# A one-core fp16x3 transformer kernel: head weight panels split ahead of the norms, the bias folded into the even low parts, and two panels given a seventh home

## The reference, cut to what matters

```python
# first block
h = x
h = h + mixed(rms_norm(h)) @ w_out                      # Hyena and mLSTM mixers
h = h + cross_attention(rms_norm(h), rms_norm(mem), wq, wk, wv, wo)
h = h + square(relu(rms_norm(h) @ ff_w1)) @ ff_w2
x = rms_norm(h, final_norm_g)
# second block, two layers (mixers differ: convolution + window attention, then GLA + MLA)
x = layer_norm(ALPHA * x + mixer(x) @ w_out, ln_mix_g, ln_mix_b)
x = layer_norm(ALPHA * x + (silu(x @ w_gate) * (x @ w_up)) @ w_down, ln_ffn_g, ln_ffn_b)
# layer_norm: ((x - mean) * rsqrt(var + eps)) * g + b ; rms_norm has neither mean nor bias
```

## Time and profile before

| | us |
|---|---|
| median of 3 runs | 2020.98 |
| the runs | 2020.11, 2020.98, 2023.48 |
| the profiled execution, its own time | 2021.97 |
| span of that execution, first to last instruction | 2020.1 |
| TensorE matmul busy | 1970.3 (98%) |
| TensorE weight load busy | 1188.0 (59%) |
| VectorE busy | 939.5 (47%) |
| ScalarE busy | 731.5 (36%) |
| GpSimd busy | 368.9 (18%) |
| mean granted TensorE clock, share of full speed | 0.993 |

### The profile page before, as it was taken

One profiled execution on the slowest core, in us unless ns is written; L12 is line 12 of the kernel. 1 busy time (PEld: TensorE's weight loads), 2 busy tenths in 40 slices (PEclk: granted clock), 3 DMA queues, 4 the chain that ended last, 5 costly groups with the idle time before them and its releaser, 6 DMA issues.

```text
span 2020.1 us, 27357 instructions
## 1 busy us (share of the span) xinstructions
PE 1970.3 (98%) x11550; PEld 1188.0 (59%) x11550; DVE 939.5 (47%) x1254; ACT 731.5 (36%) x1173; POOL 368.9 (18%) x379
## 2 busy tenths in 40 slices
PE   8999999999999999999999999999999999999997
PEld 5655555757664444885576444448766575444466
DVE  6666677645543322254745222222665663222224
ACT  6443312435343331143534222212465543322213
POOL 1011111410132210042016121200610125211100
PEclk9999999999999999999999999999998999999999
DMA  7221100332322333322121333323111022222331
GB/s 244 84 84 63 63 22 21 102 107 105 105 70 98 104 104 104 105 84 105 63 84 63 104 104 104 104 96 113 64 63 57 28 84 101 98 95 103 104 105 42
DMA packets 28228, 179.66 MB, mean 89 GB/s; under 512 B 2960, under 2 KB 7184, under 8 KB 7184
## 3 DMA queue, kind: packets, MB, share of 16 engines
q1 hardware_dynamic: 27312, 170.93, 24.5%
q10 hardware_dynamic: 512, 4.94, 0.7%
q0 software_dynamic: 288, 2.10, 0.3%
HBM read 175.86 MB, written 2.10 MB: 88 GB/s over the span
## 4 chain that ended last, share of the span: by engine, by line
PE 85%; DVE 8%; ACT 3%; POOL 1%; issue 1%; DMA 1%; SPq 0%; ACTq 0%; DVEq 0%
PE psum_a L382 25%; PE psum_a L384 25%; PE psum_a L383 25%; PE psum_a L717 2%; PE psum_b L519 2%; DVE X L1822 1%; DVE RINV L1796 1%; PE psum_a L655 1%; POOL U L2583 1%; DMA W<-weights 1%; PE psum_b L632 1%; PE psum_a L728 1%; ACT W_PARTS L1232 1%; PE psum_b L1057 1%; DVE X L1827 1%
## 5 line engine op out<-in xcount | busy, mean ns | idle before, releaser
L1802 DVE SCALAR_TENSOR_TENSOR W_PARTS<-W,W_PARTS 128x2048 f16<-128x2048 f32 x145 | 332.6, 2297 | 617.0 <-ACT W_PARTS L1232 616.9
L382 PE MATMUL psum_a<-U,W_PARTS 128*128 128x512 f16 (+1 forms) x1256 | 471.2, 375 | 2.8 <-DVE U L1816 1.8
L383 PE MATMUL psum_a<-U,W_PARTS 128*128 128x512 f16 (+1 forms) x1256 | 471.1, 375 | 0.0
L384 PE MATMUL psum_a<-U,W_PARTS 128*128 128x512 f16 (+1 forms) x1256 | 471.0, 375 | 0.0
L1232 ACT ACTIVATE W_PARTS<-W 128x2048 f16<-128x2048 f32 x145 | 275.8, 1906 | 492.7 <-PE psum_a L384 491.1
L382 PE MATMUL psum_a<-ARENA,W_PARTS 128*128 128x256 f16 (+2 forms) x956 | 295.7, 309 | 3.0 <-DVE W_PARTS L1802 3.0
L383 PE MATMUL psum_a<-ARENA,W_PARTS 128*128 128x256 f16 (+2 forms) x956 | 295.5, 309 | 0.0
L384 PE MATMUL psum_a<-ARENA,W_PARTS 128*128 128x256 f16 (+2 forms) x956 | 295.5, 309 | 0.0
L382 PEld LDWEIGHTS psum_a<-U,W_PARTS 128*128 128x128 f16 x1256 | 122.9, 98 | 150.0 <-issue 4.1
L383 PEld LDWEIGHTS psum_a<-U,W_PARTS 128*128 128x128 f16 x1256 | 122.9, 98 | 143.1 <-issue 2.9
L384 PEld LDWEIGHTS psum_a<-U,W_PARTS 128*128 128x128 f16 x1256 | 122.9, 98 | 143.1
(11 more groups left out here) (308 smaller groups left out, 2735.1 us busy)
## 6 DMA issues: line engine op xcount, KB each, us to landing
W<-weights SPq DMA_DIRECT2D x159, 1024.0 KB, 4.8
CON<-const ACTq DMA_DIRECT2D x1, 3071.5 KB, 11.0
X<-x_in SPq DMA_DIRECT2D x4, 256.0 KB, 3.9
X<-x_in SPq DMA_DIRECT2D x1, 1024.0 KB, 7.8
U<-dft POOLq DMA_DIRECT2D x1, 1024.0 KB, 5.4
ARENA<-dft POOLq DMA_DIRECT2D x1, 1024.0 KB, 5.2
U<-mem_in ACTq DMA_DIRECT2D x1, 1024.0 KB, 4.7
y_out<-U SPq DMA_DIRECT2D x2, 512.0 KB, 3.0
```

The lines of the kernel that those rows point to most:

```text
L382: nc.tensor.matmul(out, left(0), right(0), start=first, stop=False)
L383: nc.tensor.matmul(out, left(0), right(1), start=False, stop=False)
L384: return nc.tensor.matmul(out, left(1), right(0), start=False, stop=last)
L1802: nc.vector.scalar_tensor_tensor(out=home[:, 1, :], in0=W[g % 2][:, :], scalar=W_SCALE, in1=home[:, 0, :], op0=ALU.mult, op1=ALU.subtract) ...
```

## The change

Five edits.

1. A seventh home, `IN_LAST`, in the last 2048 columns of the arena. It takes the second of the two tail panels ahead of the norms ff, ln_mix0 and ln_mix1, the last down panel of each MLP, and the first query panel qx 0.
2. Both head panels of ff, final, ln_mix0, ln_ffn0, ln_mix1 are split ahead of the norm; before, the second was split between the squares and the root of the first half on ACT, and ahead of the reciprocal on DVE.
3. In three layer_norms (all but ln_ffn1) DVE makes the low part of each even tile itself, bias included, and no longer adds the bias in place; ACT makes the high part of even tiles with the bias (one instruction) and for odd tiles the high part and then x with the bias (two). POOL makes the four odd low parts of a half, and adds the bias of even tiles while it scales by ALPHA.
4. The arrivals of the second half stand behind fixed scalings: ff behind tiles 1, 3, 5; final behind 1, 4; ln_mix0 and ln_mix1 behind 1, 5; ln_ffn0 behind 4; ln_ffn1 behind 6.
5. Cross-attention: km 3 is split one place sooner (ahead of the root of the second half of norm x), qx 0 and qx 1 follow one place sooner each, and `keep_busy(9)` is gone.

```diff
+        last16 = ARENA[:, ARENA_N - PANEL:].bitcast(F16).rearrange("p (l c) -> p l c", l=2)
+        HOMES = [..., mix16w[:, 0], mix16w[:, 1], last16]
+        IN_ARENA, IN_MIX, IN_LAST = (2, 3), (4, 5), 6
...
-                    halves(q, homes=None, between=sums_between(tail))
+                    halves(q, homes=(None, IN_LAST) if tail in HEAD else None, between=sums_between(tail))
...
-            keep_busy(9)
-            project_panel("qx", 0, U16, first_wait=low_whole("x"))
+            project_panel("qx", 0, U16, first_wait=low_whole("x"), home=IN_LAST)
...
-                        w, g = panel()
+                        w, g = panel(IN_LAST if key == M.down_panels[-1] else None)
... ScalarE, norm and layer_norm
-                    if half == 0:
-                        split(head_panel(name, 1))
... ScalarE, mlp
-                used_panels(M, M.down_panels[:-2])
+                used_panels(M, M.down_panels[:-3])
+                act.wait_ge(sem(f"hidden_low_{M.name}"), 2 * M.groups)
+                used_panels(M, M.down_panels[-3:-2])
                 if M.next_norm in HEAD:
-                    split(head_panel(M.next_norm, 0))
+                    for n in range(2):
+                        split(head_panel(M.next_norm, n))
... ScalarE, layer_norm
-                        elif kt % 2:
-                            high(sem(f"biased_{name}"), 4 * half + kt // 2 + 1, U16[:, 0, kt, HALVES[half]], x, f"high_{name}")
+                        elif kt % 2 == 0:
+                            high(sem(f"gained_{name}"), 8 * half + kt + 1, U16[:, 0, kt, HALVES[half]], x, f"high_{name}", bias)
... ScalarE, cross-attention (VectorE alike)
             used(("km", 0))
+            used(("km", 1))
             root("x", 1)
...
             km_high(1)
-            used(("km", 1))
+            used(("km", 2))
             km_high(2)
-            used(("km", 2))
+            used(("km", 3))
             km_high(3)
-            used(("km", 3))
... VectorE, gain_tiles
-                        dve.wait_ge(sem(f"gained_{name}"), 8 * half + kt)
-                        nc.vector.tensor_scalar(x, x, par(BIAS[name], kt - 1), None, ALU.add).then_inc(sem(f"biased_{name}"), 1)
-                    if midway and kt == 1:
-                        midway()
+                        dve.wait_ge(sem(f"high_{name}"), 8 * half + kt)
+                        nc.vector.scalar_tensor_tensor(out=U16[:, 1, kt - 1, HALVES[half]], in0=x, scalar=par(BIAS[name], kt - 1),
+                                                       in1=U16[:, 0, kt - 1, HALVES[half]], op0=ALU.add, op1=ALU.subtract)\
+                            .then_inc(sem(f"even_low_{name}"), 1)
+                    if kt in late:
+                        late[kt]()
+            late_at = {"ff": (1, 3, 5), "final": (1, 4), "ln_mix0": (1, 5), "ln_mix1": (1, 5), "ln_ffn0": (4,), "ln_ffn1": (6,)}
... VectorE, norm
-                        if name in HEAD:
-                            split(head_panel(name, 1))
... VectorE, arrivals
-                            if q is not None:
+                            if q is not None and source == "out":
                                 used(source, q)
+                            elif q == 0:
+                                used_all(source, 2)
...
                         lists[0].insert(4, lambda: split(head_panel(name, 0)))
+                        lists[0].insert(7, lambda: split(head_panel(name, 1)))
... GpSimd
+            def odd_low(name):
+                for half in range(2):
+                    for kt in range(1, KT, 2):
+                        pool.wait_ge(sem(f"high_{name}"), 8 * half + kt + 1)
+                        nc.gpsimd.tensor_tensor(U16[:, 1, kt, HALVES[half]], in_x(kt, half), U16[:, 0, kt, HALVES[half]], ALU.subtract)\
+                            .then_inc(sem(f"low_{name}"), 1)
... GpSimd, rescale
+                    if name in NORMS_LN and kt % 2 == 0:
+                        nc.gpsimd.tensor_scalar(x, x, par(BIAS[name], kt), ALPHA, ALU.add, ALU.mult).then_inc(sem("scaled"), 1)
... GpSimd, layer_norm
-                    norm_low(name, in_x, U16)
+                    odd_low(name)
                     rescale(name)
```

More of the change, by code:

```diff
@@ L548, in low_halves, with wait @@
             def low_halves(name):
-                return lambda kt, half: pe.wait_ge(sem(f"low_{name}"), 8 * half + kt + 1)
+                def wait(kt, half):
+                    if name not in NORMS_LN:
+                        pe.wait_ge(sem(f"low_{name}"), 8 * half + kt + 1)
+                    else:
+                        pe.wait_ge(sem(f"low_{name}" if kt % 2 else f"even_low_{name}"), 4 * half + kt // 2 + 1)
+                return wait
             def low_whole(name):
@@ L1354, in layer_norm @@
                     squares(name, half, in_x, lambda kt: act.wait_ge(sem("centred"), 16 * n + 8 * half + kt + 1))
-                    if half == 0 and name in HEAD:
-                        split(head_panel(name, 1))
                     root(name, half, eps=1)
@@ L1618, in _ @@
             used_all("xo", 2)
-            split(head_panel("ff", 0))
+            for n in range(2):
+                split(head_panel("ff", n))
             norm("ff", in_x, in_nt, U16, lambda: first_tiles(FF, 0, 0))
@@ L1657, in _ @@
             used_all("eo", 2)
-            split(head_panel("ln_mix0", 0))
+            for n in range(2):
+                split(head_panel("ln_mix0", n))
             layer_norm("ln_mix0", lambda: first_tiles(GLU0, 0, 0))
@@ L1777, in _ @@
             output_high("om", 4, 4)
-            used_all("oo", 2)
-            split(head_panel("ln_mix1", 0))
+            used("oo", 0)
+            act.wait_ge(sem("gla_low"), 4)
+            used("oo", 1)
+            for n in range(2):
+                split(head_panel("ln_mix1", n))
             layer_norm("ln_mix1", lambda: first_tiles(GLU1, 0, 0))
@@ L1844, in norm @@
                             add()
-                        if name in HEAD:
-                            split(head_panel(name, 1))
                     inverse(name, half)
-                    gain_tiles(name, half, src, out, gain, second[at] if half == 0 and at + 1 < len(second) else None)
-                    if half == 0:
-                        for add in second[at + 1 if at + 1 < len(second) else at:]:
-                            add()
+                    assert half or len(late_at[name]) == len(second) - at
+                    late = dict(zip(late_at[name], second[at:])) if half == 0 else {}
+                    gain_tiles(name, half, src, out, gain, late)
             def arrivals(name):
@@ L2305, in _ @@
             inverse("x", 0)
[L2306 removed]
+            gain_tiles("x", 0, in_x, in_qx, "norm_x", {1: second[1]})
             second[2]()
@@ L2619, in mlp @@
                         .then_inc(sem(f"hidden_low_{M.name}"), 1)
+            def odd_low(name):
[4 more added lines that the diff above has]
+                            .then_inc(sem(f"low_{name}"), 1)
             def rescale(name):
                 for n in range(2 * KT):
-                    x = in_x(n % KT, n // KT)
-                    pool.wait_ge(sem(f"low_{name}"), n + 1)
-                    nc.gpsimd.tensor_scalar(x, x, ALPHA, None, ALU.mult).then_inc(sem("scaled"), 1)
+                    kt, half = n % KT, n // KT
+                    x = in_x(kt, half)
+                    if name not in NORMS_LN:
+                        pool.wait_ge(sem(f"low_{name}"), n + 1)
+                    elif kt % 2:
+                        pool.wait_ge(sem(f"low_{name}"), n // 2 + 1)
+                    else:
+                        pool.wait_ge(sem(f"even_low_{name}"), n // 2 + 1)
+                    if name in NORMS_LN and kt % 2 == 0:
+                        nc.gpsimd.tensor_scalar(x, x, par(BIAS[name], kt), ALPHA, ALU.add, ALU.mult).then_inc(sem("scaled"), 1)
+                    else:
+                        nc.gpsimd.tensor_scalar(x, x, ALPHA, None, ALU.mult).then_inc(sem("scaled"), 1)
             norm_low("mem", in_mem, MEM16)
```

15 lines of the change are left out of this document (6 added, 9 removed).

## The result

The changed kernel takes 2011.19 us in the median of five runs (2010.47 to 2013.08), the kernel before 2020.29 beside it (2020.11 to 2023.48): ratio 0.9942, 95% interval 0.9926 to 0.9958. The forecast was 2010.8 in a range of 2005.5 to 2016.3. The profiled execution took 2011.19, its span is 2009.4 (before 2021.97 and 2020.1). Measured again beside the experiments (`after_again`), on another chip: 2012.26 against 2024.29, ratio 0.9944 (0.9929 to 0.9958). Its span times its granted clock is 1994.3 in the mean of five runs, against 2007.8 in the fifteen of before there; 1994.5 to 1996 was expected, and a lucky set of clock stretches would have left less than 9 us between the two. The measure is rough (the clock is known to three digits, which is 1 us), but the gain does not rest on the clock.

What follows compares the result with a forecast made beforehand. TensorE was taken as the bound, busy 1970.3 of 2020.1 us. Terms -3.7 - 2 x 2.8 - 3.1 - 0.2 + 1.6 + 0.85 = -10.15 us, from a median of 2020.98, gave 2010.8, range 2005.5 to 2016.3.

Steps and rivals of the forecast that it cites:

- Cross-attention, -3.7: Cross-attention: km 3 starts near 411.3 us, waiting for a bank, not its split; qx 0 starts 3.7 us sooner, at 416.5.
- ln_mix0 and ln_mix1, -2.8 each: Both norms: reciprocal 1.15 us sooner, all 2.1 us of first-half delay go; 2.8 us saved each, bounds -3.2 and -1.0.
- 0.4 us stay: Second half of ln_mix0 and ln_mix1: POOL's last low part comes 7.8 us behind the reciprocal, TensorE asks at 7.4.
- ln_ffn0, -3.1: ln_ffn0: reciprocal 1.15 us sooner and the pair's addition behind tile 4 save 3.1 us, bounds -3.5 and -1.2.
- ln_ffn1, -0.2: ln_ffn1: one addition placed ahead of the eighth scaling saves 0.2 us, bounds -0.6 and +0.3.
- final, +1.6: Norm final: DVE idles 1.6 us before the last pair's addition, delaying POOL's pair sums; costs 1.6 us, bounds 0 and +2.2.
- ff, +0.85: Norm ff: the last tile's addition behind tile 5 delays two scalings by 0.8 us; costs 0.85 us, bounds -0.3 and +1.5.
- The rescaling, 0: POOL's scaling by ALPHA with two operations: up to 8.4 us more per norm, but covered, so zero cost.
- DVE is not the bound: Rival: DVE becomes the bound between the scalings, at 0.85 us an instruction beside POOL; 2034.8 us, slower; 4%.
- The layer_norms kept nothing of their waits: Rival: layer_norms keep half their waits because ACT and DVE wait for each other at each pair; 2015.2 us; 15%.
- The late additions did cost: Rival: the late additions of ff and final cost nothing, the pair sums being late anyway; 2008.3 us; 14%.
- The clock did not fall where the filler had stood: Rival: the clock falls where the cross-attention filler stood, 1.7 us a fall; 2012.5 to 2014.2 us; 10%.

Runs made afterwards that it cites:

- filler_back: The changed kernel with the nine filler matmuls put back between km 3 and qx 0: 2014.07 us, ratio 0.9950 to the kernel before.
- second_head_late: The changed kernel with each norm's second head panel split inside the norm again, on ACT and DVE: 2017.83 us, ratio 0.9970 to the kernel before.
- ln_additions_back: The changed kernel with the last pair addition of ln_mix0, ln_mix1 and ln_ffn0 behind the eighth scaling again: 2017.35 us, ratio 0.9963 to the kernel before.
- rescale_twice: The changed kernel with one more POOL multiplication by 1.0 ahead of each scaling by ALPHA: 2018.28 us, ratio 0.9972 to the kernel before.
- late_behind_eighth: The changed kernel with the last pair addition of final and ff behind the eighth scaling again: 2008.63 us, ratio 0.9922 to the kernel before.

## Why the prediction was right

- *Cross-attention, -3.7.* Measured -3.69 and, alone, -3.68. Its chain held step by step: reciprocal 2.0 us later (forecast 2.2), km 3 at 411.17 (411.3), a wait of 1.3 us for the bank (1.4), qx 0 at 416.41 (416.5). The filler is 1.94 of it (filler_back). The two decimals say more than is known: only the trace of before has the old code there, and by the distance from 376 to 425 us (52.68 in it, 47.99 to 49.02 in the nine traces with after's code) the gain lies between 3.7 and 4.7.
- *ln_mix0 and ln_mix1, -2.8 each.* Measured -3.10 and -3.11. The mechanism was right. The reciprocal's 1.15 us were worth 1.13 and 1.14 (second_head_late). The forecast counted the low parts on DVE and the additions only within the rest; they are 1.31 and 0.79. The step that was too cautious is the second half's "0.4 us stay": TensorE's waits show nothing there.
- *ln_ffn0, -3.1.* Measured -3.58, just past the bound of -3.5. The addition's 1.1 us were worth 1.32 (ln_additions_back), the reciprocal only 0.66.
- *ln_ffn1, -0.2.* Measured -0.23.
- *final, +1.6.* Measured +1.38, and the place of one addition is its cause: moving it gives 2.00 back. DVE idled 1.98 us where 1.6 was worked out, and the wait of 0.52 became 1.90 ("about 2"). *ff, +0.85*: +0.69, of which the addition's place is 0.57.
- *The rescaling, 0.* Right, but with a thinner cover than named (rescale_twice), and the operation that it bounded at 1.05 to 2.1 us takes 0.48.
- *The sum.* -10.15 against -11.6 by the stages and -10.8 between the two profiled executions. The stages' terms were too small by 1.5 us in all, and 0.8 of it went back in the clock's stretches, which no term named. So that 2010.8 comes within 0.4 us of 2011.19 is luck in part, two small errors that cancel; on the other chip the medians differ by 12.0. The range was not what it was said to be: the terms' upper ends, added up, reach 2019.3 and not 2015.2, the lower ends 2005.1.
- *The rivals.* DVE is not the bound, though 12 us follow from one more instruction a pair. The layer_norms kept nothing of their waits. The late additions did cost. The clock did not fall where the filler had stood, in any trace, but it fell behind final's wait, in seven of the nine traces with that wait. The wait was in the forecast; only the filler's place was examined for the clock.

Open stays which idle stretch brings a fall. The waits from the end of norm final to 1013 us (two of 1.7 us, one of 1.0) are the same in before, after and late_behind_eighth, and of these three only after has the fall of 6.8 us there. What differs is the time at which the same products run: those at 984 us in after come 0.7 us later in before and 4.7 us sooner in late_behind_eighth. The Trainium skill (TensorE: Matmul & The Clock Gate, section Part 1: The HAM clock gate) says that the chip judges the engine's activity on a schedule that runs freely and does not start with the kernel. These traces agree with it, with a fall of 6.8 us in one and none in the others behind the same waits, but no run here moved the program against that schedule on purpose.

## What to carry to other kernels

When an engine interleaves late work between steps that another engine waits for, ask for each inserted instruction when its operand is made: an addition whose products end 2 us later stops the whole queue behind it (+2.0 us in final), while the same edit where the operand lay ready was worth 0.8 to 1.3 us in each layer_norm. Where the runs of one kernel spread over 8 us, compare the distances between the same two instructions of the bottleneck engine, stage by stage; in the norms they repeated to hundredths and showed terms that the medians here could not. Sharing low parts out between two engines pays only while the engine that takes them keeps under the bottleneck's rate: one DVE instruction of 0.48 us more per pair took back the whole change.

## What the runs showed of the hardware that was not expected

- POOL's scaling with a pointer and two operations is faster than the one with a constant: 0.48 us against 0.84 for 128x256 fp32, and 0.45 against 0.83 from one start to the next (rows of after below). The forecast had bounded it at 1.05 to 2.1.
- POOL can stand still while DVE makes splits: the same operation takes 4.58 us, from 1091.42 to 1096.0, beside two splits on DVE that end at 1095.7 and that take their usual 2.2 to 2.3 us each. The Trainium skill (GPSIMD Engine Reference, section Specifications) names shared SBUF interfaces and contention for DVE instructions with two SBUF inputs; the split is one. The trace agrees in that the two meet; but here POOL pays and DVE does not, where before, beside POOL's low parts, DVE's scalings took 0.85 in place of 0.44 us. It is also part of why the doubled rescale took 34.4 us in place of 27.5: two of its operations take 2.32 us and one 2.82 beside splits, in place of 0.85. POOL and DVE in after:

```profile
1090.14 0.48 POOL L2655 TENSOR_SCALAR X<-X,PAR 128x256 f32<-128x256 f32 x1
1090.59 0.84 POOL L2657 TENSOR_SCALAR X<-X 128x256 f32<-128x256 f32 x1
1091.42 4.58 POOL L2655 TENSOR_SCALAR X<-X,PAR 128x256 f32<-128x256 f32 x1
```

```profile
1091.24 4.49 DVE L1812 SCALAR_TENSOR_TENSOR W_PARTS<-W,W_PARTS 128x2048 f16<-128x2048 f32 x2 [1.31 <-ACT W_PARTS L1238]
```

- Stretches at the lower clock come and go between kernels that differ by a few us ahead of them, as at 992 us, and between executions of one kernel. In the 56 runs of before beside the experiments the time spreads from 2020.2 to 2028.5 us, with a mean granted clock of 0.990 to 0.995, the lower the longer.
